# A dense norm placed beside every second RWKV projection, with four places for its input rows

## The reference

```python
# first block, after its attention and SSM paths
mix   = concat([o, y]) @ w_out
h_res = h_res + rms_norm(mix, post_mix_g)          # "mix norm", first part
h     = rms_norm(h_res, pre_ffn_g)                 # "mix norm", second part
f     = (silu(h @ w_gate) * (h @ w_up)) @ w_down
h_res = h_res + rms_norm(f, post_ffn_g)
# second block
hn   = rms_norm(h_res, norm_mix_w)
proj = hn @ w_in_2                                 # RWKV columns: 14 tiles of 128, then 4 x 512 retention columns
y_rw = rwkv7_mix(proj[..., RET_COLS:], ...)        # begins with h + (shifted h - h) * mu, tanh, sigmoid, small products
```

## Time and profile before

| | before |
|---|---|
| median of 3 runs | 3544.47 us (3542.82 to 3557.18) |
| the profiled execution: own time | 3552.9 us |
| the profiled execution: span | 3551.1 us |
| TensorE busy | 3127.4 us, 88% of the span |
| GpSimd, VectorE, ScalarE busy | 1968.9, 1733.6, 855.8 us |
| mean granted TensorE clock | 0.93 |

### The profile page before, as it was taken

How to read it: one execution, slowest core, us unless ns; L and a number is a source line. 1 busy time by engine, 2 the same in 40 slices (tenths; PEclk the granted TensorE clock), 3 DMA queues, 4 the chain that set the end, 5 groups by cost and what they waited for, 6 DMA issues and landing times.

```text
span 3551.1 us, 47884 instructions
## 1 busy us (share of the span) xinstructions
PE 3127.4 (88%) x19536; PEld 2405.1 (68%) x19536; DVE 1733.6 (49%) x2368; ACT 855.8 (24%) x1588; POOL 1968.9 (55%) x1076
## 2 busy tenths in 40 slices
PE   6987877798997859979999988988999989899997
PEld 4765645576776647767777766776777767688875
DVE  5845433334433651765666652386555564322233
ACT  3111122322222232122323223122222332200012
POOL 5711224254554636746767645665666674477873
PEclk9887988799998979999999989999999999899998
DMA  4343323122212324322222242422222222322331
GB/s 156 112 134 83 97 77 111 66 66 84 72 66 66 130 97 147 114 77 81 81 70 87 70 145 95 142 95 78 78 76 75 89 76 63 122 95 93 97 100 55
DMA packets 158028, 330.00 MB, mean 93 GB/s; under 512 B 34960, under 2 KB 74064, under 8 KB 157808
## 3 DMA queue, kind: packets, MB, share of 16 engines
q1 hardware_dynamic: 58752, 213.94, 18.7%
q10 hardware_dynamic: 99056, 112.99, 9.9%
HBM read 281.89 MB, written 44.97 MB: 92 GB/s over the span
## 4 chain that ended last, share of the span: by engine, by line
PE 75%; DVE 16%; ACT 3%; ACTq 2%; issue 2%; DMA 2%; DVEq 0%
PE ps L1783 30%; PE ps L1812 12%; PE ps L1824 12%; PE ps L1637 2%; PE ps L1548 2%; DVE acc_dense L2224 1%; DVE ffh_lo L2909 1%; PE ps L1518 1%; DVE act_lo L2224 1%; DVE xn_dense L2231 1%; PE ps L2023 1%; ACTq L937 1%; PE ps L1558 1%; PE ps L1665 1%; PE ps L1717 1%
## 5 line engine op out<-in xcount | busy, mean ns | idle before, releaser
L537 POOL TENSOR_TENSOR w_hi<-w_raw,ones 128x1024 fp32r<-128x1024 f32 x408 | 796.5, 1952 | 1305.5 <-DMA w_raw<-weights 1302.5
L539 POOL TENSOR_TENSOR w_lo<-w_raw,w_hi 128x1024 fp32r<-128x1024 f32 x408 | 1004.7, 2462 | 32.0
L1783 PE MATMUL ps<-act_hi,w_hi 128*128 128x512 f32 x1696 | 706.1, 416 | 7.2 <-DVE act_lo L2224 6.6
L1783 PE MATMUL ps<-act_lo,w_hi 128*128 128x512 f32 x1696 | 680.2, 401 | 0.0
L1783 PE MATMUL ps<-act_hi,w_lo 128*128 128x512 f32 x1696 | 676.1, 399 | 0.0
L1783 PEld LDWEIGHTS ps<-act_hi,w_hi 128*128 128x128 f32 x1696 | 325.4, 192 | 99.3 <-issue 15.5
L1783 PEld LDWEIGHTS ps<-act_hi,w_lo 128*128 128x128 f32 x1696 | 324.9, 192 | 75.5
L1783 PEld LDWEIGHTS ps<-act_lo,w_hi 128*128 128x128 f32 x1696 | 324.9, 192 | 67.2 <-issue 1.7
L2224 DVE TENSOR_TENSOR acc_dense<-acc_dense,ps 128x512 f32<-128x512 f32 x352 | 241.9, 687 | 236.5 <-PE ps L1812 176.3
L1812 PE MATMUL ps<-w_hi,ffh_hi 128*128 128x512 f32 x704 | 296.4, 421 | 54.8 <-DVE acc_dense L2224 53.6
L1812 PE MATMUL ps<-w_hi,ffh_lo 128*128 128x512 f32 x704 | 283.1, 402 | 0.0
(11 more groups left out here) (374 smaller groups left out, 4465.3 us busy)
## 6 DMA issues: line engine op xcount, KB each, us to landing
w_raw<-weights SPq DMA_DIRECT2D x408, 512.0 KB, 3.5
rw<-rw_t ACTq DMA_DIRECT2D x24, 256.0 KB, 2.4
rw<-lora_t ACTq DMA_DIRECT2D x24, 256.0 KB, 2.0
row<-x ACTq DMA_DIRECT2D x8, 512.0 KB, 3.7
row_dense<-x ACTq DMA_DIRECT2D x8, 512.0 KB, 3.5
res<-row_dense ACTq DMA_DIRECT2D x8, 512.0 KB, 2.6
row_mix<-res ACTq DMA_DIRECT2D x8, 512.0 KB, 7.9
res<-row_mix ACTq DMA_DIRECT2D x8, 512.0 KB, 2.9
```

Source lines behind the costliest of these rows:

```text
L537: pool.tensor_tensor(w_hi[:, s], raw, ones[:, 0:1].to_broadcast([P, 1024]), MUL).then_inc(w_hi_made, 1)
L539: pool.tensor_tensor(w_lo[:, s], raw, w_hi[:, s].bitcast(F32), SUB).then_inc(w_ready, 1)
L1783: mm = pe.matmul(out, ws[w][:, s, P * k:P * k + P], acts[a][:, k, x], start=(k, w, a) == (0, 0, 0), stop=(k, w, a) == (KT - 1, 1, 0))
```

## The change

Phase 2 places only the 32 product steps behind the residual's steps, and one norm step behind each of the projections n = 0, 2, 4, 6, 8 and 10. Since `acc_mix` now lives through the projections, the six buffers of `rw_projection` move by 16 KB. In half 1 the input rows 2 and 3 get two places of their own (`row_more`), and are loaded in norm step 0, with no wait for a store; they signal on `out_landed[2]` and `out_landed[3]`, which is why the later wait on these counts one load more. Half 0 of the norm keeps its two places and its order.

```diff
+    row_more = place("row_more", [P, 2, D], F32, AT_MIX + 32768)
+    row_of = lambda h, k: row_more[:, k - 2] if h and k >= 2 else row_dense[:, k % 2]
...
-    rw_t = place("rw_t", [P, 2, BANK], F32, AT_MIX)
-    lora_t = place("lora_t", [P, 2, BANK], F32, AT_MIX + 4096)
+    rw_t = place("rw_t", [P, 2, BANK], F32, AT_MIX + 16384)
+    lora_t = place("lora_t", [P, 2, BANK], F32, AT_MIX + 20480)
...
-             2: fills([10, 8, 6, 6, 4, 4], [0] * RW_TILES, len(first_starts)),
+             2: fills([8, 8, 6, 6, 4, 0], [1, 0] * NORM_STEPS + [0] * (RW_TILES - 2 * NORM_STEPS), len(first_starts)),
...
         def load_input(h, k):
             r0 = P * (HALF * h + k)
-            act.dma_start(row_dense[:, k % 2], t["x"][r0:r0 + P, :]).then_inc(x_landed[k % 2], 16)
+            act.dma_start(row_of(h, k), t["x"][r0:r0 + P, :]).then_inc(out_landed[k] if h and k >= 2 else x_landed[k % 2], 16)
...
             for step in range(NORM_STEPS):
+                if h and step == 0:
+                    for k in (2, 3):
+                        load_input(h, k)
...
-                    act.dma_start(t["res"][r0:r0 + P, :], row_dense[:, k % 2]).then_inc(res_stored[k % 2], 16)
+                    act.dma_start(t["res"][r0:r0 + P, :], row_of(h, k)).then_inc(res_stored[k % 2], 16)
...
-                    if k < 2:
+                    if k < 2 and h == 0:
                         act.wait_ge(dense_xn, gx + k + 1)
-                        act.wait_ge(res_stored[k], 16 * (2 * h + 1))
+                        act.wait_ge(res_stored[k], 16)
                         load_input(h, k + 2)
...
-                    dve.wait_ge(x_landed[k % 2], 16 * (2 * h + k // 2 + 1))
+                    if h and k >= 2:
+                        dve.wait_ge(out_landed[k], 16)
+                    else:
+                        dve.wait_ge(x_landed[k % 2], 16 * (2 * h + k // 2 + 1))
...
-                            dve.wait_ge(out_landed[k], 16 * (h + 1))
+                            dve.wait_ge(out_landed[k], 16 * (h + 1 + k // 2))
```

More of the change, by code:

```diff
@@ L323, in build @@
     gain_post_mix = (place("gain_post_mix", [P, D], F32, AT_KEEP), gain_dense)
-    rw_t = place("rw_t", [P, 2, BANK], F32, AT_MIX)
-    lora_t = place("lora_t", [P, 2, BANK], F32, AT_MIX + 4096)
[L327 to L330, removed]
+    rw_t = place("rw_t", [P, 2, BANK], F32, AT_MIX + 16384)
+    lora_t = place("lora_t", [P, 2, BANK], F32, AT_MIX + 20480)
+    wa = place("wa", [P, BANK], F32, AT_MIX + 24576)
+    sgd = place("sgd", [P, BANK], F32, AT_MIX + 26624)
+    lora_w = place("lora_w", [P, 4 * P], F32, AT_MIX + 28672)
+    lora_g = place("lora_g", [P, 4 * P], F32, AT_MIX + 30720)
     before_half = place("before_half", [P, RW_TILES], F32, AT_KEEP + 4096)
@@ L1005, in mix_norm @@
                     r0 = P * (HALF * h + k)
-                    act.dma_start(t["res"][r0:r0 + P, :], row_dense[:, k % 2]).then_inc(res_stored[k % 2], 16)
+                    act.dma_start(t["res"][r0:r0 + P, :], row_of(h, k)).then_inc(res_stored[k % 2], 16)
                     ss = small[:, 148 + k:149 + k]
-                    give(fn(squares_first[:, :], row_dense[:, k % 2], ACT.Square, accum_out=ss), act_step)
+                    give(fn(squares_first[:, :], row_of(h, k), ACT.Square, accum_out=ss), act_step)
                     give(fn(ss, ss, ACT.Ln, bias=eps_col, scale=1.0 / D), act_step)
@@ L2568, in mix_norm @@
                     k = step
-                    dve.wait_ge(x_landed[k % 2], 16 * (2 * h + k // 2 + 1))
+                    if h and k >= 2:
+                        dve.wait_ge(out_landed[k], 16)
+                    else:
+                        dve.wait_ge(x_landed[k % 2], 16 * (2 * h + k // 2 + 1))
                     take(mix_root)
                     stt(total[:, k], total[:, k], small[:, 152 + k:153 + k], gain_post_dense[:, :], MUL, MUL)
-                    tt(row_dense[:, k % 2], row_dense[:, k % 2], total[:, k], ADD, mix_final)
+                    tt(row_of(h, k), row_of(h, k), total[:, k], ADD, mix_final)
                 if 1 <= step <= HALF:
@@ L2577, in mix_norm @@
                         dve.wait_ge(dense_turned, gt_ + k - 1)
-                    stt(xn_dense[:, k % 2], row_dense[:, k % 2], small[:, 148 + k:149 + k], gain_dense[:, :], MUL, MUL, dense_xn)
+                    stt(xn_dense[:, k % 2], row_of(h, k), small[:, 148 + k:149 + k], gain_dense[:, :], MUL, MUL, dense_xn)
                 if step >= 2:
```

## The result

The changed kernel took 3577.36 us (median of 9 runs, 3571.93 to 3589.69). The kernel before, run beside it and counted with its earlier runs, took 3555.99 us (9 runs, 3542.82 to 3567.54). The ratio is 1.0070, with a 95% interval of 1.0052 to 1.0087: slower, by 21.4 us between the medians.

What follows compares the result with a forecast made beforehand. TensorE's waits were taken to bound the kernel, with phase 2's norm-only stretch the target. Projections starting 31.1 us earlier but taking 143.0 instead of 91.8 us gave +20.1 on 3544.5: 3565 us, range 3550 to 3580.

Steps and rivals of the forecast that it cites:

- Differences are added to the median: Base of the whole sum: differences reckoned against the profiled execution were added to the shown median of 3544.47 us.
- Residual and products: Phase 2 before the projections: terms +4.95, -8.3, +2.8 and 3.3 us; projections start 31.1 us earlier.
- The first wait: TensorE ahead of the first transposes, eight products instead of ten before them: wait grows from 1.36 to 4.2 us.
- The second wait: TensorE ahead of the second transposes in phase 2: stays at 7.87 us, its chain moving by 4.95 us.
- The norm beside the projections: Phase 2 projections: 39.1 us standing, 3.5 transposes, 8.6 lower clock; stretch grows from 91.8 to 143.0 us.
- GpSimd's share in a place: VectorE slowed beside GpSimd's split in phase 2's norm steps: +1.0 us a place, bounds 0 and 5.
- The free projection covers nothing.: Phase 2: the projection between two norm steps covers none of the root's chain, only what follows it.
- T + 6.4: Phase 2, even n: the root ends 6.4 us after projection end T, 1.3 less than phase 3's 7.7.
- What costs nothing: Phase 2: some nine more ScalarE table loads, 1.28 us each, add nothing outside the chain; no drain counted.
- the norm vanishing under the projections: Rival for phase 2: TensorE never stands beside the projections; -27.6 us, 3517; chance 0.06.
- standing as in phase 3: Rival for phase 2: 2.2 us standing a place, more at the first; -11.1 us, 3533; chance 0.06.
- the cheap edges: Rival within the forecast's mechanism: no GpSimd slowing, clock holds at 4.2 us; about +14, 3559; no separate chance.

Runs made afterwards that it cites:

- e3: The changed kernel with one norm step behind each of the first six projections instead of every second one; 3577.44 us, ratio 1.0079 to the kernel before.
- e1: The changed kernel with TensorE's transposes of the half 1 mix norm one norm step later; 3531.22 us, ratio 0.9939 to the kernel before.
- e7: The changed kernel with transposes one norm step later and a norm step behind each of the first six projections; 3546.67 us, ratio 0.9984.
- e2: As e1, with the transposes of phase 3's norm beside projections also one step later; 3510.96 us, ratio 0.9891 to the kernel before.
- e5: The changed kernel's order of work with the old two input row places, loads behind stores again; 3585.71 us, ratio 1.0081 to the kernel before.
- e4: The changed kernel's four row places and product spacing, but the whole norm ahead of the first projection as before; 3546.63 us, ratio 0.9983.
- e6: The changed kernel with the row's part of each half 1 norm step ahead of the product tile's part on ScalarE and VectorE; 3569.11 us, ratio 1.0024.

## Why the prediction was right and where it was wrong

**The step that failed is the base of the sum.** The differences came to +20.1 us and phase 2 showed +19.8. But I added them to 3544.47, the median of three runs. The same kernel's median was 3555.99 over 9 runs (those three among them), and 3552.75 and 3554.81 over 13 and 20 others, and the profiled execution whose rows the whole sum uses had itself taken 3552.9. From that execution the sum gives 3573.0, 4.4 under the 3577.36 measured, and from the median of nine 3576.1, 1.3 under; from the median of three it gave 3565, 12 under. The step is "Differences are added to the median": the time of the profiled execution and the median that stood there differed by 8.4 us, and nothing in the text asked which one the new runs would repeat. The time stayed in the range of 3550 to 3580 by 2.6 us only. The chances suffered less from this than from the threshold: +20.1 lay 2.4 us beyond 17.7, so I left a third to "within 0.5%", and the measured ratio, 1.0070 with at least 1.0052, lies beyond it.

**That phase 2 came out to 0.3 us is partly luck.** Two misses of the sum cancelled: the projections started 1.7 us earlier than forecast, and their stretch was 1.4 us longer. The parts follow.

**Residual and products**, counted from 1224.6 in the old trace and 1228.4 in the new: they ended 2.4 us earlier (1295.44 - 3.8 = 1291.6 against 1294.0), where I had 0.6.
- The first wait was 4.07 us (I had 4.2), and the clock did fall: the product matmuls up to 1248.4 took 0.63 us instead of 0.39. Transposes and 8 products took 13.81 us (12.42 + 1.39), at full clock 0.87 + 8 x 1.39 = 12.0, so 1.8 in place of 2.15.
- The second wait did not stay at 7.87; it was 10.02. I had moved the chain to the second transposes, and forgot that product 15 is now the last ahead of them: before, TensorE had two more products, 2.8 us, to do in that wait. The sum was hardly touched, since it went by the transposes: they came 3.7 us later where I had 4.95, 0.6 of this from a VectorE step that now took 1.29 instead of 1.91.
- The wait of 6.17 us ahead of the last transposes went, as forecast.
- From the last product to the first projection 3.37 us (I had 3.3). Projections started 32.8 us earlier (31.1).

**The norm beside the projections.** The stops were 9.71 + 0.72, 10.53, 10.59 and 7.91 us, 39.5 in all; I had 10.6, 10.4, 10.4 and 7.7, 39.1. GpSimd's share in a place was right, in a step other than in the earlier trace rows: `acc_mix` at n = 4 took 2.40 us beside the split instead of 1.28, +1.1 (I had +1.0). But the +1.0 was only picked between bounds of 0 and 5, so that it fits is in part luck. The transposes took 4 x 1.97 us and the four projections behind them 27.6 instead of 4 x 5.77: together 12.4 for transposes and clock, where I had 3.5 + 8.6. The stretch was 144.4 us, with 143.0 forecast.

**"The free projection covers nothing."** This step was wrong in size: as e3 shows, it covers the load of Sigmoid, 1.28 us. In the sum it did no harm, since the 1.3 us were taken off there ("T + 6.4").

**What costs nothing.** The nine more table loads (155 in all) cost TensorE nothing outside the chain: it stood 39.5 us in the stretch, and the five waits named above make 39.5. None of them was for weights. The Trainium skill (ScalarE: Activation LUTs, section What ACT_TABLE_LOAD costs) has a drain of some 1380 ns besides the load. This case's trace disagrees. The chain at n = 4 leaves no room for it on either side: the load starts at 1348.17, 0.02 us behind the issue that ended at 1348.15, and the Square starts at 1349.47. Four drains would have been 5.5 us more, and the four stops summed to within 0.4 us of a forecast that had none.

**The rivals.** The first one, the norm vanishing under the projections at -27.6 us, needed roots ready before the transposes ask for them. The changed kernel doesn't have that, e1 does, and it gained 26.9 us. I had seen the condition and put it down as a fact of the engines' order, where it was one line in TensorE's own. The second, standing as in phase 3 (13.3 us in four waits there), did not come about: the waits were three times as long. Nor did the third, the cheap edges: GpSimd did slow VectorE and the clock did fall.

## What to carry to other kernels

When work is folded between steps of another kind, ask for each piece in which step its producer finishes, on which queue and behind what; if the consumer stands in the same step, the whole chain stands open, however idle the engines are. Moving the consumer one step on took nothing else with it and decided the sign here: +19.8 us became -26.9. It is enough as long as a round of the producers is no longer than the consumer's own work between two pieces; in e7 the round took 12.2 us against 7.7, and the waits came back. And add differences to a base that is as well known as they are: these were right to 0.3 us, in part by luck, and a median of three runs was 8 to 12 us under those of 9, 13 and 20.

## What the runs showed that I had not expected

Executions of the same code differ by more than the parts of this change. The nine traces run through the same program up to phase 2, and reached its first product matmul between 1220.9 (e2) and 1241.4 us (e5); the kernel before's own times went from 3542.82 to 3567.54. They differ long before the change: from 300 to 400 us the granted clock was 0.88 in e2 and 0.78 in e5, with TensorE busy for 82.3 and 80.1 of 100 us. Whether that is cause or consequence was not found; why the executions differ stays open. Local stretches spread less: the local differences of phase 2 (e1 -26.9, e4 -7.6, e5 +27.1, e6 +10.3) agree with those of the medians (-21.5, -6.1, +30.9, +14.3) to some 5 us. But they spread too. The same code of phase 3 took 112.3 to 112.5 us in the changed kernel, e1 and e7, and 115.1 to 115.6 in the traces of before, e3, e4, e5 and e6. In each of these eight traces TensorE has three waits of 2.21 to 2.24 us there; in the five longer ones the transposes behind one of the three took 1.95 to 1.97 us, in the other three always 1.09 or 1.10. So behind the same short wait the clock fell in 5 of 24 cases, and cost some 3 us when it did.

How much a VectorE step loses beside a GpSimd split follows a simple sum. In phase 2 of all nine traces a 128x1024 step of VectorE that began while a split was running took its length alone, plus what was left of the split, less 0.14 to 0.21 us (nothing, where 0.1 us or less was left). At n = 4 of the changed kernel (timelines of GpSimd and VectorE):

```profile
1350.27 2.34 POOL L541 TENSOR_TENSOR w_lo<-w_raw,w_hi 128x1024 fp32r<-128x1024 f32 x1
...
1351.31 2.38 DVE L2236 SCALAR_TENSOR_TENSOR acc_mix<-acc_mix,small,gain_post_dense 128x1024 f32<-128x1024 f32 x1 [4.73 <-ACT small L654]
```

The split ended at 1352.61, 1.30 us behind the start of the step: 1.28 + 1.30 - 0.20 = 2.38. The same sum gives the 1.63 and 2.22 us of two `acc_mix` steps of e1 (0.55 and 1.14 us left of the split), and 3.25 for the 1.23 us step of e7 (2.16 left, less 0.14). A third `acc_mix` step of e1, of 1.29 us, began 0.65 us behind the end of a split. A step that was already running when the split began kept its length, and the split grew: in e1 `row_more` took 1.23 us from 1357.30, and the split that began at 1357.77 took 2.51 us instead of 1.89. So a chain of such steps can be costed to some 0.1 us, if one knows where the splits lie.
